# The chunked recurrence of a hybrid decoder layer: the second half's logs, scan, gates and scaled keys computed beside the first half's last levels

## The reference

```
log_f = logaddexp(log(lb), log1p(-lb) + log_sigmoid(fr))   # one layer: lb = 0, so min(fr,0) - ln(1+exp(-|fr|))
kb = (1 - lb) * sigmoid(-fr);  qh = silu(qb)
b = cumsum(log_f) in each chunk
att[t,s] = sum_k q[t,k] k[s,k] exp(b[t,k] - b[s,k]),  s <= t
o = att @ v + (q * exp(b)) @ S
S_new = exp(b_last) * S + (k * exp(b_last - b))^T @ v
o = rmsnorm(o) * silu(gb)
```

## Time and profile before

| | us |
|---|---|
| median of 3 runs | 1920.42 |
| lowest, highest | 1918.97, 1920.47 |
| the profiled execution | 1917.37 |
| its span | 1915.7 |
| TensorE busy | 1857.2 (97%) |
| VectorE busy | 999.1 (52%) |
| ScalarE busy | 568.0 (30%) |
| GpSimd busy | 423.0 (22%) |

### The profile page before, as it was taken

The page is one execution under the profiler, slowest core; times in us unless marked ns, Lnnn a source line. Parts: engine busy times, 40 slices in busy tenths (PEclk is TensorE's granted clock), DMA queues, the critical chain, the costliest instruction groups (busy, mean ns, idle before and its releaser), DMA issues.

```text
span 1915.7 us, 28620 instructions
## 1 busy us (share of the span) xinstructions
PE 1857.2 (97%) x11857; PEld 1791.7 (94%) x11857; DVE 999.1 (52%) x1170; ACT 568.0 (30%) x764; POOL 423.0 (22%) x213
## 2 busy tenths in 40 slices
PE   8999998999999999999999999999999999999998
PEld 5899897897778999999899999999999999999998
DVE  6922374734674212121534866766766676685522
ACT  4234423215563211111434221221231131133610
POOL 2323222121121212221321221121121121122221
PEclk9999999999999999999999999999999999999999
DMA  5211212134324122212311110110111011011121
GB/s 198 37 67 67 68 56 88 46 124 136 111 83 146 53 82 90 78 67 99 115 67 56 67 44 22 66 55 16 61 55 44 33 65 44 22 67 45 42 79 45
DMA packets 54294, 134.26 MB, mean 70 GB/s; under 512 B 12834, under 2 KB 28738, under 8 KB 51906
## 3 DMA queue, kind: packets, MB, share of 16 engines
q1 hardware_dynamic: 42114, 105.40, 16.2%
q0 software_dynamic: 5184, 19.01, 3.1%
q10 hardware_dynamic: 6912, 8.65, 1.3%
HBM read 110.82 MB, written 22.31 MB: 69 GB/s over the span
## 4 chain that ended last, share of the span: by engine, by line
PE 91%; DVE 3%; ACT 2%; issue 2%; DMA 1%; POOL 0%; ACTq 0%; SPq 0%; POOLq 0%; DVEq 0%
PE ps L703 60%; PE ps L1120 10%; PE ps L685 8%; PE pst L1120 3%; PE ps L666 2%; PE ps L848 2%; PE ps L769 1%; PE ps L927 1%; PE ps L961 1%; PE pst L948 1%; PE ps L672 1%; DVE Ml L2021 0%; DMA masks<-in_wb 0%; PE ps L826 0%; DVE Fl L2028 0%
## 5 line engine op out<-in xcount | busy, mean ns | idle before, releaser
L2253 POOL TENSOR_TENSOR Ul<-BIG,Uh 128x1024 fp32r<-128x1024 f32 x60 | 145.2, 2419 | 710.4 <-ACT Uh L1562 630.7
L703 PE MATMUL ps<-Nh,Uh 128*128 128x352 f32 x1248 | 271.2, 326 | 4.3 <-issue 2.2
L703 PE MATMUL ps<-Nh,Ul 128*128 128x352 f32 x1248 | 269.4, 323 | 0.0
L703 PE MATMUL ps<-Fl,Uh 128*128 128x352 f32 x1248 | 269.4, 324 | 0.0
L703 PEld LDWEIGHTS ps<-Nh,Uh 128*128 128x128 f32 x1248 | 213.0, 189 | 5.8 <-issue 5.6
L703 PEld LDWEIGHTS ps<-Nh,Ul 128*128 128x128 f32 x1248 | 214.7, 188 | 0.0
L703 PE MATMUL ps<-Hh,Uh 128*128 128x352 f32 x936 | 203.8, 326 | 9.6 <-DVE Ml L2021 4.3
L703 PEld LDWEIGHTS ps<-Fl,Uh 128*128 128x128 f32 x1248 | 212.6, 188 | 0.0
L703 PE MATMUL ps<-Hh,Ul 128*128 128x352 f32 x936 | 202.2, 323 | 0.0
L703 PEld LDWEIGHTS ps<-Hh,Uh 128*128 128x128 f32 x936 | 159.7, 190 | 12.3 <-issue 5.0
L2047 DVE TENSOR_TENSOR BIG<-BIG,ps 128x1056 f32<-128x1056 f32 x32 | 40.1, 1254 | 232.1 <-PE ps L703 225.8
(11 more groups left out here) (318 smaller groups left out, 3119.9 us busy)
## 6 DMA issues: line engine op xcount, KB each, us to landing
BIG<-in_wu SPq DMA_DIRECT2D x44, 512.0 KB, 3.8
H<-in_wd SPq DMA_DIRECT2D x11, 1024.0 KB, 4.8
BIG<-in_wgl SPq DMA_DIRECT2D x20, 512.0 KB, 4.5
BIG<-in_x SPq DMA_DIRECT2D x16, 528.0 KB, 5.7
gates<-BIG ACTq DMA_DIRECT2D x48, 176.0 KB, 1.9
BIG<-in_wz POOLq DMA_DIRECT2D x16, 512.0 KB, 3.9
BIG<-gates SPq DMA_DIRECT2D x12, 528.0 KB, 3.6
BIG<-in_wge POOLq DMA_DIRECT2D x12, 512.0 KB, 3.8
```

The costliest lines, as they stand in the source:

```text
L703: ins = nc.tensor.matmul(psb(3 * out + g), w[wp][:, k], x[xp][k][:, t0:t0 + n], start=(k == 0 and wp == xp), stop=(k == kk - 1 and wp == 1))
L2253: nc.gpsimd.tensor_tensor(Ul[:, half], uraw[:, half], Uh[:, half].bitcast(F32), ALU.subtract)\
```

## The change

Half 1's preparation is split up and moved. Its logs (`next_logs`) go to rows `KF[:, 1]` behind level 5's copy-out on ScalarE, its sigmoids (`next_gates`) to `KF[:, 1]` and `QF[:, 0]` behind that of level 6; the mask goes to `QF[:, 1]`; VectorE scans, multiplies the gates and takes the chunk differences before half 0's output is there, and the scaled keys right behind reading that output. The squares and reciprocal roots use `oN = QF[:, 0]` instead of `bE`. TensorE turns half 1's keys (`turned_k(1)`) right behind half 0's head mean, one piece moves from `out0` to `start1`, and the head mean waits only for the copy-out of the last piece in bank 5. VectorE's `sample_states` of half 0 comes behind the scaled keys, so the outputs made from it are stored later. The wait for `states_stored` ahead of the sample rows of half 1 goes; the scaling ahead of them has the same wait.

```diff
-PLACES = (("states0", 2), ("levels0", 8), ("out0", 3), ("start1", 4), ("states1", 2), ("levels1", 8), ("out1", 2),
+PLACES = (("states0", 2), ("levels0", 8), ("out0", 2), ("start1", 5), ("states1", 2), ("levels1", 8), ("out1", 2),
...
+        oN = QF[:, 0]
...
-                pe.wait_ge(S("b_pre"), 7 * i + 7)
+            def turned_k(i):
+
+                pe.wait_ge(S("b_pre"), (7, 13)[i])
+                if i:
+                    pe.wait_ge(S("b_oread"), 1)
...
-                pe.wait_ge(S("gate_out"), parts(f"out{i}")[-1] + 1)
-                whole(1, cc("headmean"), bE).then_inc(S("b_ms"), 1)
+                pe.wait_ge(S("gate_out"), max(p for p in parts(f"out{i}") if fill_bank(p) == 5) + 1)
+                whole(1, cc("headmean"), oN).then_inc(S("b_ms"), 1)
+                if i == 0:
+                    turned_k(1)
...
+            def next_logs():
+
+                x = KF[:, 1]
+                act.wait_ge(S("b_adone"), 4 * 6)
+                act.wait_ge(S("b_sdone"), 2)
+                link(nc.scalar.activation(x, FB[:, 1], ACT.Abs))
+                link(nc.scalar.activation(x, x, ACT.Exp, scale=-1.0))
+                nc.scalar.activation(x, x, ACT.Ln, bias=1.0).then_inc(S("b_acts"), 1)
+
+            def next_gates():
+
+                act.wait_ge(S("b_pre"), 8)
+                nc.scalar.activation(FB[:, 1], FB[:, 1], ACT.Sigmoid, scale=-1.0).then_inc(S("b_acts"), 1)
+                nc.scalar.activation(KF[:, 1], QB[:, 1], ACT.Sigmoid).then_inc(S("b_acts"), 1)
+                act.wait_ge(S("b_adone"), 4 * 7)
+                act.wait_ge(S("b_sdone"), 4)
+                nc.scalar.activation(QF[:, 0], Z[:, GB + 1, :], ACT.Sigmoid).then_inc(S("b_acts"), 1)
+                act.preload_act_table_set("natural_log_exp_and_others")
...
+                if i == 0:
+                    act.wait_ge(S("b_pre"), 12)
+                    nc.scalar.activation(bE, bd_, ACT.Exp, scale=-1.0).then_inc(S("b_acts"), 1)
...
+                if i == 0:
+                    gate_out(parts("out0")[0])
+                    nc.scalar.activation(QE, b, ACT.Exp).then_inc(S("b_acts"), 1)
+                    act.wait_ge(S("b_states"), DB)
+                    chunk_decays()
+                    gate_out(parts("out0")[1])
...
+                    if i == 0 and l == NL - 1:
+                        ones(QF[:, 1])
                     select(l - 1)
...
+                    if i == 0 and l == NL - 1:
+                        decay_logs(1, KF[:, 1])
+                if i == 0:
+                    decay_sums(QF[:, 1])
+                    gated(1, KF[:, 1], QF[:, 0])
+                    chunk_differences()
+                else:
+                    sample_states()
...
+                if i == 0:
+                    dve.sem_inc(S("b_oread"), 1)
+                    dve.wait_ge(S("b_acts"), 13)
+                    v.tensor_tensor(bE, bE, FB[:, 1], ALU.mult).then_inc(S("b_pre"), 1)
+                    sample_states()
                 dve.wait_ge(S("b_rs"), i + 1)
                 dve.wait_ge(S("states_stored"), i + 1)
-                link(v.scalar_tensor_tensor(gg, gg, pc("hgrn_norm"), bE, ALU.mult, ALU.mult))
+                link(v.scalar_tensor_tensor(gg, gg, pc("hgrn_norm"), oN, ALU.mult, ALU.mult))
```

More of the change, by code:

```diff
@@ L819, in _ @@
                     ins.then_inc(S("b_tdone"), 1)
+            turned_k(0)
+            for i in range(2):
+                if i:
+                    for p in parts("start1"):
+                        if p == parts("start1")[0]:
+                            pe.wait_ge(S("b_rs"), 1)
+                        fill(p)
                 pe.wait_ge(S("b_tfree"), 3 * i + 3)
-                pe.wait_ge(S("b_pre"), 7 * i + 6)
+                pe.wait_ge(S("b_pre"), (6, 14)[i])
                 if i:
@@ L1351, in gate_out, with before @@
                     .then_inc(S(f"gate_stored{p % 2}"), 16)
[L1354 to L1364, removed]
+            def before():
+                f, q, g = FB[:, 0], QB[:, 0], Z[:, GB, :]
+                act.wait_ge(S("d_rows"), 16)
+                for user in ("FB0", "QB0", "GB0"):
+                    z_wait(user)
+                for user in ("FB1", "QB1", "GB1"):
+                    z_wait(user)
                 link(nc.scalar.activation(bE, f, ACT.Abs))
@@ L1367, in before @@
                 nc.scalar.activation(bE, bE, ACT.Ln, bias=1.0).then_inc(S("b_acts"), 1)
[L1368 to L1371, removed]
+                act.wait_ge(S("b_pre"), 1)
                 nc.scalar.activation(f, f, ACT.Sigmoid, scale=-1.0).then_inc(S("b_acts"), 1)
@@ L1412, in exponents @@
                     nc.scalar.activation(ev[:, :, 1, :], dv[:, :, 1, :], ACT.Exp).then_inc(S("b_exps"), 1)
+                if i:
+                    for p in parts("start1"):
+                        gate_out(p)
                 exponents(0, LEVELS[0])
@@ L1845, in _, with ones @@
[L1845 to L1852, removed]
+                def ones(rmask):
+                    link(v.memset(rmask, 1.0))
+                    link(v.memset(rmask[:, 0:SEQ:CH], 0.0), v.memset(rmask[:, SEQ:T:DL], 0.0))
@@ new lines, in chunk_differences, with sample_rows @@
+                def chunk_differences():
+                    link(v.tensor_tensor(dp, bp, bp[:, :, CH - 1:CH].to_broadcast([P, NCH, CH]), ALU.subtract),
+                         v.tensor_tensor(dss, bs, bs[:, :, DL - 1:DL].to_broadcast([P, DB, DL]), ALU.subtract))
+                    dve.sem_inc(S("b_pre"), 1)
+                def sample_rows(n):
+                    dve.wait_ge(S("vt_free"), 6)
+                    for bb in range(DB):
+                        ins = v.tensor_scalar(vbd[0:NS, bb, :], VT[0:NS, NCH, HW + n * P:HW + n * P + P],
+                                              cc("batch", 1, bb, NS), None, ALU.mult)
+                        link(ins)
+                    dve.sem_inc(S("b_pre"), 1)
@@ L1854, in _ @@
                 dve.wait_ge(S("b_u"), i + 1)
[L1855 removed]
+                dve.wait_ge(S("b_acts"), 16 if i else 7)
                 dve.wait_ge(S("vt_free"), 12)
@@ L1931, in _ @@
                         factors(l, LEVELS[l])
-                sample_states()
+                    if i == 0 and l == NL - 1:
[3 more added lines that the diff above has]
+                    gated(1, KF[:, 1], QF[:, 0])
+                    chunk_differences()
+                else:
+                    sample_states()
                 dve.wait_ge(S("b_odone"), i + 1)
```

80 lines of the change are left out of this document (43 added, 37 removed).

## The result

| | before | after |
|---|---|---|
| median, us | 1920.45 | 1907.53 |
| lowest, highest | 1918.97, 1920.66 | 1906.33, 1909.8 |
| profiled execution, its span | 1917.37, 1915.7 | 1906.33, 1904.6 |
| mean granted clock of that execution | 0.994 | 0.998 |

The changed kernel takes 0.9927 of the time (interval 0.9915 to 0.9939), 12.9 us less by the medians. The gain forecast was 9.5.

The account below looks back on a forecast made before the run. TensorE, busy 97% of the span, bounds the kernel; the edit is worth its waits plus their clock cost. Gains of 7.43, 0.64 and 2.07 less 0.6 make 9.5 us: median 1910.9, range 1907.6 to 1916.6.

Parts of the forecast that it names:

- The mechanism: Preparing half 1's keys early, ahead of half 0's output, removes TensorE's wait for them at L817.
- The long wait: TensorE's wait at L817 for VectorE's scaled keys of the second half goes: 7.43 us gained.
- head mean: First half's head mean no longer waits, the last piece ahead lying in the other bank: 0.64 us gained.
- the side chain: Half 1's logs, scan, sigmoids, products and keys on ScalarE and VectorE finish at 301.7, 4.9 us before TensorE asks.
- The keys were not late: Rival, 0.05: logs, scan, products and exponentials slow down beside the levels and GpSimd's splits; at twice their time, 1927.4.
- given back: Rival, 0.08: later levels, norms and attention, bound by queues, wait for what comes 9.5 us earlier; about 1920.
- the turned keys: Ninth transpose waits for ScalarE's copy behind the roots: 3.4 us added, 2.80 of before gone, a cost of 0.6.
- the sum: Terms 7.43 + 0.64 + 2.07 - 0.6 = 9.5 us gained, all up to the end of the second half's state products.
- The products run at full clock: Second half's state products, L826 and L830, take 3.96 us instead of 6.03 at the lower clock: 2.07 gained.
- low end: Lowest earlier run, 1918.97, less 9.5 and less 1.9 for the factors' waits, should they shift: 1907.6.
- waits of the factors: Two TensorE waits, 1.9 us, at first levels behind the factors; forecast to stay, taken off only at the range's bottom.
- The clock rival: Rival, 0.20: clock falls at the new pause behind the head mean, following pieces lose 3.4 us: 1914.3.

Follow-up runs that it names:

- the keys turned late: Changed kernel with three pieces at out0 and four at start1 again, half 1's keys turned at their old place behind start1: 1909.0 us, ratio 0.9927.
- both pairs of profiles: Recorded pair, then both kernels run and profiled again without edit: before 1921.34 us, changed 1908.68 us, ratio 0.9934.
- partly filled wait: Kernel before with 26 constant matmuls where TensorE waited 7.4 us for the second half's keys: 1918.3 us, ratio 0.9981.
- the pieces back: Changed kernel with three pieces at out0 and four at start1, as in the kernel before: 1912.12 us, ratio 0.9947.
- the long pause: Changed kernel with four more ScalarE copies ahead of its copy of the turned keys, lengthening TensorE's pause: 1918.9 us, ratio 0.9976 of before.
- filled wait: Kernel before with 32 constant matmuls in the wait for the second half's keys, TensorE busy to its end: 1915.42 us, ratio 0.9972.
- the norms filled: Constant matmuls put in the waits of the norms, in either kernel: kernel before 0.9992, changed kernel 0.9923 of before.

## Why the prediction was right or wrong

**The mechanism was right.** The long wait went, its place was taken by a wait of 2.0 us for ScalarE at the ninth transpose, the head mean lost its 0.64, and the side chain was 5.4 us early where I had 4.9. The keys were not late in any profile, and nothing of the gain was given back, since the rest is shorter too. That the early preparation alone gives it is shown by the keys turned late.

**The terms, in the one pair of profiles.** The stretch gained 10.53, of which: wait 7.43 (forecast 7.43), head mean 0.64 (0.64), products from 5.97 to 3.78, 2.19 (2.07), the turned keys 3.29 for 2.80, a cost of 0.49 (0.6), and the seven pieces, 27.89 to 27.13 as what is left over, 0.76 that I did not have. That is 1.0 us over the forecast of 9.5. Three sums of the prediction are slightly off and change nothing: 279.43 + 0.46 + 0.4 + 3 times 1.09 is 283.6, not 283.7; 4.9 - 1.58 is 3.3, not 3.4, so the cost comes to 0.5; and 303.9 + 4.8 is 308.7, not 309.5. Of the 0.76, 0.3 is a matter of counting: a wait is counted from the modelled end of the last matmul, 0.32 behind its start, where the next one would follow after 0.16, and two such waits are gone. Another 0.2 lies at the first piece behind the head mean, whose second matmul starts 0.43 behind the first; in the changed kernel, where it stands behind the transposes, it is 0.24. The other 0.3 stays open.

**The step that failed** is the sum: its terms are "all in TensorE's time up to the end of the second half's state products", and all that comes behind was put at nothing, with no case but a loss. In both pairs of profiles what comes behind is shorter, by 2.2 us in the first and 2.0 in the second. In the norms it is 1.5 and 1.1 (50.75 and 50.16 against 49.23 and 49.09), the low window that only the kernel before has. From the last L1051 to the end it is 1.2 and 0.7. Of that 0.7 stands between all profiles with one low window in this part, with or without the change (1313.1 against 1312.4), and its cause is open; the other 0.5 of the first pair is a low window near 1785, which the first profile of the changed kernel lacks. The parts between differ by 0.5 the other way in the first pair and by 0.2 in the second.

The norms' low window was in my rows, and I used it as evidence for a rival, not as a part of the kernel's time. In the profiles whose norms were left alone, five have a low window between 300 and 353 (before twice, the partly filled wait, the pieces back, the long pause), and all five have one in the norms; five have none there (changed twice, filled wait, late turn, split turn), and none of them in the norms. That the two go together is shown in these ten; how one brings the other is not. Low windows near 230 and from 1772 to 1790 come and go without regard to either.

**The second step** is the clock's term, "The products run at full clock", with its 2.07. For the profile on which it was worked out it is right: the wait filled with work gives 46.31 - 43.43 = 2.9 us for the clock, and 2.07 with the 0.8 by which the turned keys ran slower (2.80, against 1.99 from 336.93 to 338.92 with the wait filled) is 2.9 too. But another execution pays 47.76 - 43.43 = 4.3. The three profiles of the kernel before, the third with the norms filled, have stretches of 46.31, 47.76 and 47.77, according to whether the clock is back by 342 or at 353, while those of the changed kernel agree within 0.06. So the term was 1.45 too small for the second kind of execution, and the forecast for the median took the first kind; how many executions are of which is not known. Of the 5.2 us between the first two profiles of the kernel before, only this 1.45 goes with the stall; 3.8 lie ahead of L882, where the changed kernel's two profiles also stand 3.15 apart, and taking the gain off the median was right for them.

For the second pair of profiles the account is: up to L882 1.0 lost, the stretch 47.76 - 35.78 = 12.0 gained, the rest 1572.45 - 1570.45 = 2.0 gained, 13.0 in all, the difference of the medians of these runs being 12.7.

**The range.** Its low end took 1.9 us for the waits of the factors, which stayed (1.9 in the rows of after), and nothing for the clock, which entered the high end only. With the products at half speed throughout, as in the second profile of before (7.42 - 3.78 = 3.64 instead of 2.07), the low end would have been 1.6 lower and the result inside. The rest, put at nothing, would have done the same.

**The clock rival** had 0.20 and did not happen in any of the three profiles in which the single pause of 1.96 us stands (the changed kernel twice, and once with the norms filled). It did in the one profile with 0.65 us of waiting 5 us ahead of the same pause. There the low window cost 1.8 in the stretch and 1.1 in the norms; that the whole kernel was 3.4 slower, the rival's price, is luck, since 0.65 of it is the wait. My evidence against the rival, that the first half's transposes kept the clock at 1.00, was that of one execution: six of the thirteen profiles have a low window there. TensorE's waits ahead of it are 0.76, 0.30, 0.25 and 0.36 us within 3.3 us in the second profile of the kernel before, and 0.75, 0.30, 0.25 and 0.36 in the first, in which the clock stayed up. The Trainium skill, "TensorE: Matmul & The Clock Gate", section "A second HAM failure mode: psum-queue depth-cycling", says that idling shortly and often between groups of matmuls makes the clock go back and forth. The six windows near 230 fit that, the seven profiles without one show that it is not certain, and a single pause is not what that section describes, though the prediction took it so.

## What to carry to other kernels

A stall of TensorE had three prices here: its length, 7.4 us; the work behind it at half speed, 2.9 to 4.3; and a low window later on, in the norms, 1.0 to 1.5, whose link with the stall is seen in ten profiles but not explained. A single profile shows the clock's share of one execution, so before a term of the clock is taken from it, see how the mean granted clock spreads over the executions, and cut two profiles of the same kernel at the same instructions to see in which part they differ. A stall that can't be removed can be filled: constant matmuls into a free bank gave back half of what the whole rearrangement did.

## What had not been expected of the hardware

The return from the half clock took 7 us in one execution and 15 in another, of the same instructions (L817 at 334.39 and full clock by 342; L817 at 338.23 and some 353). Two waits of 0.65 and 1.96 us within 5 us of each other were followed by a mean granted clock of 0.57 over 4 us, where the 1.96 alone left it at 1.00 in three profiles; that is one profile, and chance is not ruled out. With the wait partly filled, a pause of 1.63 us and one of 0.36 were enough: L829 behind them took 3.48 us instead of 2.05. Low windows near 230 us, in code that no experiment changed, come in six of thirteen profiles, and L882 then starts at 300.69 to 301.67 instead of 296.85 to 299.59.
